# Rows of the later expert slots fetched from DRAM by token number, in place of one-hot gathers on TensorE

## The reference, cut to what matters

```python
def moe_ffn(h, router, w1, w3, w2):
    logits = (h @ router).astype(jnp.float32)
    top_v, top_i = lax.top_k(logits, TOP_K)              # TOP_K = 2
    top_w = jax.nn.softmax(top_v, axis=-1)
    gates = jnp.sum(jax.nn.one_hot(top_i, N_EXPERTS) * top_w[..., None], axis=-2)
    y = gates[..., 0:1] * swiglu(h, w1[0], w3[0], w2[0])
    for e in range(1, N_EXPERTS):
        y = y + gates[..., e:e + 1] * swiglu(h, w1[e], w3[e], w2[e])
    return y                                              # swiglu: (silu(h@w1) * (h@w3)) @ w2
# the caller: h = rmsnorm(x, g_ffn[1]); x = x + moe_ffn(h, ...); return rmsnorm(x, g_final)
```

## Time and profile before

| | |
|---|---|
| median of 3 runs | 1487.76 us (1483.42 to 1487.79) |
| profiled execution | 1485.04 us, of which the span of instructions is 1482.6 us |
| granted TensorE clock | 0.999 of full speed |
| TensorE matmul busy | 1463.4 us (99% of the span) |
| VectorE, ScalarE, GpSimd busy | 895.5, 712.8, 20.6 us |
| DMA over the span | 471.40 MB, mean 318 GB/s |
| queue of the expert weights, whole span | 78.9% of 16 engines |

### The profile page before, as it was taken

The page is one execution under the profiler, slowest core; times in us unless marked ns, Lnnn a source line. Parts: engine busy times, 40 slices in busy tenths (PEclk is TensorE's granted clock), DMA queues, the critical chain, the costliest instruction groups (busy, mean ns, idle before and its releaser), DMA issues.

```text
span 1482.6 us, 19448 instructions
## 1 busy us (share of the span) xinstructions
PE 1463.4 (99%) x7738; PEld 1096.6 (74%) x7738; DVE 895.5 (60%) x901; ACT 712.8 (48%) x752; POOL 20.6 (1%) x39
## 2 busy tenths in 40 slices
PE   9999999999999999999999999999999999999997
PEld 8888889999998888853588834688634888888633
DVE  5856776555457577740399700798402997998402
ACT  5564645434353646420387500677202876877201
POOL 2000000000000000000000000000000000000000
PEclk9999999999999999999999999999999999999999
DMA  9654455555475544799999999999999999999896
GB/s 327 226 163 157 162 179 171 188 182 195 147 248 186 173 165 143 266 408 426 427 426 427 426 426 426 427 427 426 427 427 426 426 427 427 412 379 358 344 427 288
DMA packets 106977, 471.40 MB, mean 318 GB/s; under 512 B 7932, under 2 KB 12160, under 8 KB 63888
## 3 DMA queue, kind: packets, MB, share of 16 engines
q1 hardware_dynamic: 103664, 460.11, 78.9%
q0 software_dynamic: 2656, 9.51, 2.0%
q10 hardware_dynamic: 576, 0.61, 0.1%
HBM read 469.15 MB, written 2.10 MB: 318 GB/s over the span
## 4 chain that ended last, share of the span: by engine, by line
PE 86%; DMA 8%; ACT 2%; SPq 2%; DVE 1%; issue 1%; DVEq 0%; POOL 0%; POOLq 0%
PE big L1900 13%; PE big L1895 13%; PE big L1896 13%; PE big L2459 11%; DMA eraw<-experts 7%; PE small L1895 5%; PE small L1896 5%; PE small L1900 5%; PE big L1974 4%; PE big L1981 4%; PE big L1975 4%; PE small L2002 2%; PE small L2459 2%; SPq L667 1%; PE big L2355 1%; DMA raw<-w_gate 1%
## 5 line engine op out<-in xcount | busy, mean ns | idle before, releaser
L1275 DVE TENSOR_TENSOR elo<-eraw,ehi 128x2048 fp32r<-128x2048 f32 x168 | 379.9, 2288 | 49.3 <-ACT ehi L1006 35.3
L1006 ACT ACTIVATE ehi<-eraw 128x2048 fp32r<-128x2048 f32 x164 | 314.5, 1919 | 128.3 <-PE small L1900 59.5
L1179 DVE TENSOR_TENSOR wlo<-raw,whi 128x2048 fp32r<-128x2048 f32 (+2 forms) x104 | 229.8, 2217 | 136.8 <-ACT whi L784 135.9
L784 ACT ACTIVATE whi<-raw 128x2048 fp32r<-128x2048 f32 (+2 forms) x103 | 190.8, 1857 | 223.7 <-PE big L1900 79.8
L2459 PE MATMUL big<-eraw,he 128*64 128x512 f32 (+1 forms) x1024 | 196.6, 541 | 0.5 <-DVE he L1795 0.5
L1895 PE MATMUL big<-ehi,hehi 128*128 128x512 f32 x448 | 176.0, 393 | 1.9 <-ACT ehi L1003 1.9
L1896 PE MATMUL big<-ehi,helo 128*128 128x512 f32 x448 | 174.4, 389 | 0.0
L2459 PEld LDWEIGHTS big<-eraw,he 128*64 128x64 f32 x1024 | 71.7, 137 | 116.5 <-issue 107.5
L1895 PE MATMUL big<-whi,hhi 128*128 128x512 f32 (+1 forms) x384 | 152.1, 396 | 0.0
L1896 PE MATMUL big<-whi,hlo 128*128 128x512 f32 (+1 forms) x384 | 149.0, 388 | 0.0
L1852 DVE TENSOR_TENSOR hid<-hid,big 128x512 f32<-128x512 f32 (+1 forms) x16 | 9.9, 621 | 195.2 <-PE big L2459 195.2
(11 more groups left out here) (375 smaller groups left out, 1828.2 us busy)
## 6 DMA issues: line engine op xcount, KB each, us to landing
eraw<-experts SPq DMA_DIRECT2D x336, 1024.0 KB, 20.2
raw<-ffn_w SPq DMA_DIRECT2D x30, 1024.0 KB, 5.0
raw<-w_gate SPq DMA_DIRECT2D x24, 1024.0 KB, 5.0
raw<-w_in SPq DMA_DIRECT2D x19, 1024.0 KB, 5.3
raw<-w_branch SPq DMA_DIRECT2D x12, 1024.0 KB, 5.0
raw<-w_o SPq DMA_DIRECT2D x8, 1024.0 KB, 5.0
raw<-w_in SPq DMA_DIRECT2D x4, 896.0 KB, 10.5
gbias<-b_gate POOLq DMA_DIRECT2D x12, 256.0 KB, 4.6
```

The lines of the kernel that those rows point to most:

```text
L784: act.activation(whi[u % HI][:, 0:kt, 0:cols], raw[u % RAW][:, 0:kt, 0:cols], ACT.Copy).then_inc(hi_ready, 1)
L1006: act.activation(ehi[HI_OF[n]][:, :], eraw[n % RING][:, :], ACT.Copy).then_inc(ehi_ready, 1)
L1179: dve.tensor_tensor(wlo[u % RAW][:, 0:kt, 0:cols], raw[u % RAW][:, 0:kt, 0:cols], whi[u % HI][:, 0:kt, 0:cols].bitcast(F32), ALU.subtract) ...
L1275: dve.tensor_tensor(elo[n % RING][:, :], eraw[n % RING][:, :], ehi[HI_OF[n]][:, :].bitcast(F32), ALU.subtract).then_inc(elo_ready, 1)
```

## The change

- ScalarE writes xn = X * nrs (the normalised rows) in two instructions, one per block of 128 tokens, before it takes the exponents.
- GpSimd copies the 256 rows of `xn` (1 MB) to a DRAM tensor `xrows`.
- Slot 0 is gathered as before (`first_gather`). For each later slot: `Gm` is now plain one-hot (is_equal alone). After n = 26 (`NUMBERED`) TensorE multiplies `Gm` with a column of token numbers (`rows_numbered`), into `small[:, 2, 0:1]`: the number of the token at each place, and 0 for a place without a token. At n = 28 VectorE turns them into integers (`numbers_taken`, `rowi`). GpSimd then issues an indirect DMA (`rows_in`), which fetches the rows with these numbers from `xrows` into `xs`, which is `xn[:, 0, :]`: 64 rows for slots 2 and 4, 128 rows for slots 1, 3, 5, 6 and 7.
- `gather` waits for that DMA and then makes 8 transposes of 128 features each.
- Results are added into `X` (there is no `ACC`), and the last normalisation goes into `xn`, from where it is written out.
- TensorE waits for `rows_ready` before it writes bank 2 of `small` at n = 31.

```diff
@@ -113,7 +113,8 @@
-PICKED, GATED, GATES_TURNED, GATES_TAKEN = 24, 1, 36, 41
+PICKED, NUMBERED, NUMBERS_TAKEN = 24, 26, 28
+GATED, GATES_TURNED, GATES_TAKEN = 1, 36, 41
 HE = 2 * PAIRS - 1
...
@@ -376,7 +378,7 @@
         GT32 = at("GT32", over_mask + 6144, [SLOT, NB, P])
-        ACC = xn
+        xs = xn[:, 0, :]
         place[0] = work + o
@@ -395,6 +397,8 @@
         gcol = keep("gcol", [P, 1])
+        mark = keep("mark", [P, 1])
+        rowi = keep("rowi", [P, 1], I32)
         need = keep("need", [P, NM])
...
@@ -542,6 +552,8 @@
+        xrows = nc.dram_tensor("xrows", [TOKENS, D], F32, kind="Internal")
         w_in, w_gate, w_branch, w_o = ins["w_in"], ins["w_gate"], ins["w_branch"], ins["w_o"]
@@ -678,7 +690,7 @@
                 sp.wait_ge(x_ready, 12 + 2 * b + 2)
-                sp.dma_start(out[0, b * P:(b + 1) * P, 512:1024], X[:, b, 512:1024]).then_inc(out_done, 16)
+                sp.dma_start(out[0, b * P:(b + 1) * P, 512:1024], xn[:, b, 512:1024]).then_inc(out_done, 16)
             sp.wait_ge(out_done, 16 * 2 * NB)
@@ -738,6 +750,27 @@
+            for b in range(NB):
+                pool.wait_ge(xn_ready[b], 1)
+                pool.dma_start(xrows[b * P:b * P + P, :], xn[:, b, :]).then_inc(rows_out, 16)
+            pool.tensor_tensor(mark[:, :], eps[:, :], eps[:, :], ALU.add).then_inc(marked, 1)
+            def rows_in(s):
+                n = CAP if is_light(s) else SLOT
+                pool.indirect_dma_start(xs[0:n, :], None, xrows[:, :],
+                                        bass.IndirectOffsetOnAxis(ap=rowi[0:n, 0:1], axis=0)).then_inc(xs_in, 16)
+            pool.wait_ge(rows_out, 16 * NB)
+            for s in range(1, LOOP + 1):
+                pool.wait_ge(rows_ready, s)
+                rows_in(s)
+            pool.wait_ge(routed, 1)
+            last = pool.value_load(metai[0:1, SLOTS:SLOTS + 1], min_val=NE - 1, max_val=SLOTS - 1)
+            with pool.Fori(LOOP + 1, last + 1) as s:
+                pool.wait_ge(marked, s - LOOP)
+                pool.wait_ge(rows_ready, s)
+                pool.tensor_tensor(mark[:, :], eps[:, :], eps[:, :], ALU.add).then_inc(marked, 1)
+                rows_in(s)
@@ -1118,6 +1151,10 @@
             act.activation(nsd[:, 3, :], nvar[:, 3, :], ACT.Sqrt, scale=1.0 / D, bias=eps[:, :]).then_inc(sd_ready, 1)
+            act.wait_ge(rs_ready, 4)
+            for b in range(NB):
+                act.activation(xn[:, b, :], X[:, b, :], ACT.Copy, scale=nrs[:, 3, b:b + 1]).then_inc(xn_ready[b], 1)
             act.wait_ge(lmax_ready, 1)
@@ -1147,14 +1184,14 @@
                 part = slice(512 * half, 512 * half + 512)
-                a = act.activation(X[:, b, part], ACC[:, b, part], ACT.Square, accum_out=nss[:, 4, half, b:b + 1])
+                a = act.activation(xn[:, b, part], X[:, b, part], ACT.Square, accum_out=nss[:, 4, half, b:b + 1])
                 if half:
...
                 act.wait_ge(x_ready, 12 + 2 * b + 1)
-                act.dma_start(out[0, b * P:(b + 1) * P, 0:512], X[:, b, 0:512]).then_inc(out_done, 16)
+                act.dma_start(out[0, b * P:(b + 1) * P, 0:512], xn[:, b, 0:512]).then_inc(out_done, 16)
             act.wait_ge(out_done, 16 * 2 * NB)
@@ -1634,8 +1671,14 @@
                 for b in range(NB):
-                    i = dve.tensor_scalar(Gm[:, b, :], iota, cq[:, 0, b:b + 1], nrs[:, 3, b:b + 1], ALU.is_equal, ALU.mult)
+                    i = dve.tensor_scalar(Gm[:, b, :], iota, cq[:, 0, b:b + 1], None, ALU.is_equal)
                 i.then_inc(picked_ready, 1)
+            def numbers_taken(s):
+                dve.wait_ge(numbered, s)
+                dve.tensor_copy(rowi[:, :], small[:, 2, 0:1]).then_inc(rows_ready, 1)
@@ -1670,10 +1713,9 @@
                     dve.wait_ge(spread_done, 2 * s + b + 1)
-                old = X if isinstance(s, int) and s == 0 else ACC
                 for half in range(2):
                     part = slice(512 * half, 512 * half + 512)
-                    i = dve.tensor_tensor(ACC[:, b, part], old[:, b, part], big[half][:, 1, :], ALU.add)
+                    i = dve.tensor_tensor(X[:, b, part], X[:, b, part], big[half][:, 1, :], ALU.add)
                 i.then_inc(final_added if final else spread_added, 1)
@@ -1684,6 +1726,8 @@
                     picked(s + 1)
+                if n == NUMBERS_TAKEN and not final:
+                    numbers_taken(s + 1)
                 if n in SPREAD_ADDED and not (isinstance(s, int) and s == 0):
...
@@ -1880,7 +1924,7 @@
                 for part in (slice(0, 512), slice(512, 1024)):
-                    dve.scalar_tensor_tensor(X[:, b, part], ACC[:, b, part], nrs[:, 4, b:b + 1], gfin[:, part], ALU.mult,
+                    dve.scalar_tensor_tensor(xn[:, b, part], X[:, b, part], nrs[:, 4, b:b + 1], gfin[:, part], ALU.mult,
                                              ALU.mult).then_inc(x_ready, 1)
@@ -2343,17 +2387,34 @@
+            def first_gather():
+                pe.wait_ge(picked_ready, 1)
+                for j in range(2):
+                    for k in range(4):
+                        for b in range(NB):
+                            f = (4 * j + k) * P
+                            i = pe.matmul(big[j][:, 1, CAP * k:CAP * k + CAP], X[:, b, f:f + P], Gm[:, b, 0:CAP], start=b == 0,
+                                          stop=b == NB - 1)
+                    i.then_inc(gather_done, 1)
+            def rows_numbered(s):
+                pe.wait_ge(picked_ready, s + 1)
+                for b in range(NB):
+                    i = pe.matmul(small[:, 2, 0:1], Gm[:, b, :], tab[:, T_TOK + b:T_TOK + b + 1], start=b == 0, stop=b == NB - 1)
+                i.then_inc(numbered, 1)
             def gather(s, rows):
-                pe.wait_ge(picked_ready, s + 1)
+                pe.wait_ge(xs_in, 16 * s)
                 if not (isinstance(s, int) and s < 2):
...
                     for k in range(4):
-                        for b in range(NB):
-                            f = (4 * j + k) * P
-                            i = pe.matmul(big[j][:, 1, rows * k:rows * k + rows], X[:, b, f:f + P], Gm[:, b, 0:rows], start=b == 0,
-                                          stop=b == NB - 1)
+                        f = (4 * j + k) * P
+                        i = turn(big[j][:, 1, rows * k:rows * k + rows], xs[0:rows, f:f + P], rows)
                     i.then_inc(gather_done, 1)
@@ -2409,6 +2470,10 @@
                     i.then_inc(eunit_done, 1)
+                    if n == NUMBERED:
+                        pe.wait_ge(alo_ready, HE * wides_before(s) + 3)
+                        rows_numbered(s + 1)
                     if n == GATES_TURNED:
@@ -2420,6 +2485,9 @@
                             pe.wait_ge(gt_ready, s)
+                        elif t == 4:
+                            pe.wait_ge(rows_ready, s + 1)
                         if t == HE - 1:
@@ -2463,6 +2531,10 @@
                     d.then_inc(eunit_done, 1)
+                    if n == NUMBERED and not final:
+                        pe.wait_ge(light_taken, PAIRS * i + 2)
+                        rows_numbered(s + 1)
                     if n == GATES_TURNED:
@@ -2474,12 +2546,15 @@
                                 pe.wait_ge(gt_ready, s)
+                            elif p == 2 and not final:
+                                pe.wait_ge(rows_ready, s + 1)
                             for j in range(light_width(p) // P):
...
-            gather(0, CAP)
+            first_gather()
             for s in range(LOOP):
@@ -2523,6 +2598,7 @@
+    t[:, T_TOK:T_TOK + NB] = i[:, None] + P * np.arange(NB)[None, :]
     t[:, T_SUM:T_SUM + NE] = i[:, None] % COLS == np.arange(NE)[None, :]
```

More of the change, by code:

```diff
@@ L157 @@
 T_SUM = T_SIN + NB * ROPE // 2
-T_W = T_SUM + NE
+T_TOK = T_SUM + NE
+T_W = T_TOK + NB
 MIX_UNITS = 34
@@ L512, in encoder @@
         picked_ready = sem("picked_ready")
+        xn_ready = [sem(f"xn_ready{b}") for b in range(NB)]
+        rows_out = sem("rows_out")
+        numbered = sem("numbered")
+        rows_ready = sem("rows_ready")
+        marked = sem("marked")
+        xs_in = sem("xs_in")
         light_turned = sem("light_turned")
@@ L1871, in _ @@
                 dve.wait_ge(end_spread, i + 1)
-                part = ACC[:, b, 512 * half:512 * half + 512]
+                part = X[:, b, 512 * half:512 * half + 512]
                 dve.tensor_tensor(part, part, big[half][:, b, :], ALU.add).then_inc(end_added, 1)
```

## The result

The changed kernel took 1490.67 us (median of 12 runs, 1487.44 to 1502.75); the kernel before, run beside it, 1485.11 us. The ratio is 1.0046 (95% interval 1.0025 to 1.0067). The forecast was 1490.2 us with a range of 1484.5 to 1497.0. So the time lies 0.5 us from the forecast, and the loss is real. What has to be tested is whether the reasons hold.

What follows compares the result with a forecast made beforehand. Bytes were taken to bound the kernel up to slot 5, TensorE behind it. -4.5 us from TensorE and +6.9 from DMA gave +2.4 on 1485.04 (1487.4), plus 2.7 to the median: 1490.2 us, range 1484.5 to 1497.0.

Steps and rivals of the forecast that it cites:

- What bounds the kernel: Bytes at 427 GB/s set the pace up to slot 5's first unit (1143.6 us), TensorE behind it.
- TensorE's saving: Cheaper gathers save 2.25 us a slot, counting only in slots 5 and 6: -4.5 us (3.6 to 5.4).
- The bytes: Copies and gathers in the saturated stretch make slot 5 start 6.9 us later (4.9 to 9.8).
- the price taken half-way to POOL's queue: 1.4 us per 128 fetched rows, between 1.23 at the weights' rate and 1.63 at the POOL queue's rate.
- The copies: Writing `xn` to DRAM at about 647 to 652 us: 2.8 us, partly hidden in unused time, so +1.3 (0 to 3.3).
- What lies beside: Waits for numbers, descriptors and landing rows cost nothing: 27.1 us are left in wide slots, 18.6 in light ones.
- Behind slot 5: Gathers for slots 6 and 7 (2 x 1.4 us) fit into 18.7 us of unused transfer time: no cost.
- Rival 1: Added packets fill gaps left at 427 GB/s, slot 5 starts on time: 1483.3 us; chance 0.08.
- Rival 2: A fetched row costs DMA engines far more than a copied one, at twice the price 1498.6 us; chance 0.20.
- its threshold of 1.75: Price in us per 128 rows from which the kernel would be measurably slower.
- Rival 3: VectorE shuts GpSimd out while descriptors are made, rows come late; at 35 us, 1506.0 us; chance 0.07.
- The marks: Signs: 0.9 us transposes, DMA share 1.01, slot 5 near 1150 us, TensorE idle 5 us before it, POOL up 4.2 MB.

Runs made afterwards that it cites:

- nofetch: The changed kernel without the copy to DRAM and without any fetch, transposes reading rows of tokens 0 to 127: 1482.31 us.
- slowpe: The changed kernel with the eight transposes of the gathers for slots 1 to 5 made four times over: 1491.06 us.
- hybrid: The changed kernel with one-hot gathers from `xn` for slots 1 to 5, fetches for slots 6 and 7 only, copy put off to slot 5: 1481.52 us.
- double: The changed kernel with each fetch issued twice, the second into the other half of `xn`: 1499.16 us.
- hot: The changed kernel with all row numbers made 0, so each fetch reads the same 4 KB repeatedly: 1490.53 us.
- distinct: The changed kernel with each place's row number replaced by the place's own number, so all rows differ and are in order: 1489.18 us.
- halfrow: The changed kernel with plain loads of 128 rows of 2 KB into all 128 partitions for slots 1 to 5: 1485.44 us.
- alldirect: The changed kernel with each indirect fetch replaced by a plain load of the same number of rows: 1490.63 us.

## Why the prediction was right, and where it was not

**The number: closer than the sum deserved.** The 1490.2 us add +2.4 to 1487.76 us, the median of three executions of the kernel before. Twelve executions beside the changed kernel gave 1485.11. So the base was 2.65 us too high and the loss 3.2 us too low (5.6 by the medians; by the ratio, into which the three long executions count, 6.8, with an interval of 3.7 to 10.0), and the two misses offset each other. Inside the profiled execution the stage accounts for +3.0, near the sum's +2.4; the other 2.6 us of the spans stand ahead of the first gather and are not explained.

**What bounds the kernel: right.** Two pieces, bytes up to slot 5 and TensorE behind it. nofetch and slowpe show both sides of the first piece: cheaper gathers leave the pair at 207, and 11.9 us more of TensorE's work leaves it at 210. The second piece is 244.7 to 244.8 us in hybrid, nofetch, double and slowpe, whatever happens ahead of it.

**TensorE's saving: right, a little high.** Forecast 2.25 us a slot, measured 4.23 / 2 = 2.12. The chain of waits after, the view that gave the forecast's prices, has the numbering (forecast 0.45) and the eight transposes (0.87) of slot 6:

```profile
1352.91 0.34 PE small L2406 x4
...
1380.68 0.88 PE big L2046 x8
```

By these a slot would save 3.57 - 0.34 - 0.88 = 2.35 us, so neither price was too low, and where the 0.2 us to the measured 2.12 go is not shown.

**The bytes: near in the sum, by errors that offset each other.** Forecast +6.9 us up to slot 5; measured 2.15 + 2.77 + 2.71 = +7.6. The step that failed is the one that counted rows: 128 + 64 + 128 + 64 + 128 = 512 rows as four blocks of 1.4 us. A block of 128 rows costs 1.26 us, its bytes at the full rate (1.23), so the price taken half-way to POOL's queue was too dear. And a block of 64 rows is no half of it but 1.28 us: there are five blocks, not four, 3 x 1.26 + 2 x 1.28 = 6.3 us for 5.6. The copies cost 0.9 for 1.3. That makes 7.2; the 0.4 us left are within what pairs differ by from run to run (209.8 to 210.4 among the kernels with 64-row fetches). The section of the Trainium skill on the ports, named above, would have given the fifth block; I read the earlier trace rows for the price of a byte and did not ask where the bytes land. The forecast's range also had no case for an execution that runs at 388 GB/s for 100 us: 1498.78 and 1502.75 lie above its 1497.0, though the median hardly moves with them.

**What lies beside: right.** Rows land after 9.7 us (forecast 9.9 to 13.3) of the 18.6 that a light slot leaves. VectorE waits 1.47 us for the numbers ahead of its copy in slot 1, as costed (1.3):

```profile
811.98 0.16 DVE L1681 CAST rowi<-small 128x1 int32<-128x1 f32 x1 [1.47 <-PE small L2406]
```

**Behind slot 5: right.** The fetches for slots 6 and 7 cost nothing (hybrid against nofetch), and slot 7 moved with slots 5 and 6; the end is 0.4 us shorter, not longer.

**Rival 1, bytes absorbed: refuted.** They cost 7.6 us up to slot 5 in the profile, and the medians of hybrid and nofetch lie 9.2 and 8.4 us under that of the changed kernel. **Rival 2, a fetched row is dear: refuted as put** (hot and distinct have the same pair; 1.26 us for 128 rows is under its threshold of 1.75), with a grain of truth in the 64-row blocks at 1.28 us for half the rows. **Rival 3, rows late: its mechanism is real and its effect nil.** GpSimd makes a fetch in 0.94 us in light slots and in 2.7 us in wide ones, where VectorE's subtractions with two SBUF inputs run; 5.8 us were allowed for, and 27.1 us were free. The Trainium skill ("SBUF — State Buffer", section "Who interferes with whom") says that such a VectorE instruction and a GpSimd one that reads SBUF contend, by an exclusive lock; the trace agrees: the fetch begun at 812.41 us ended at 815.14, 0.8 us after the first of two subtractions of 2.29 us that began at 812.05. The plain transfers of halfrow and alldirect, which read no numbers, were made in 0.52 to 0.58 us beside the same subtractions.

**The marks.** The DMA share stayed at 1.01, the eight transposes took 0.88 us in the chain (forecast about 0.9), the queue of POOL took 4.2 MB more (2.8% of 1488.2 less 2.0% of 1482.6 us is 12 us, 1.5 us for each 0.52 MB). Slot 5 came at 1153.87, 3.9 us later than the 1150 named: 2.6 of these are the start of that execution. The idle time of TensorE, forecast as 5 us or more ahead of slot 5, came apart, 0.5 us at each of the last light units and 1.59 us at the start, since TensorE overtakes the loads already inside the light slot.

## What to carry to other kernels

Ask of each stretch which resource ends it, and move work only into the stretch where the other one is idle: the same edit is worth +2.7 us a pair before slot 5 and -2.1 us a slot behind it, and the version that makes it only behind (1481.52 us) beats both kernels. Price an added transfer into saturated engines by the partitions that it fills as well as by its bytes: here 64 rows of 4 KB took the time of 128, and long slow stretches came only with such fetches. When a number comes out right, look at the base and at the terms apart, by marks inside one execution; here a base that was too high hid part of the loss, and two wrong terms offset each other.

## What the hardware showed that was not expected

- With a 64-row fetch in the stream of weights, 16 engines at a share of 1.01 moved 416 to 418 GB/s over 40 us for 426 to 427, the packets of the weights took longer beside it too, and in some executions 388 GB/s for 100 us, worth 8 to 10 us of the time (two of them profiled).
- The clock of TensorE is not the same in all executions of one kernel. Stretches of nofetch where slot 0 starts, and then those of before:

```profile
640.00:645.00 5.00, 4.08 (x23) 2.04 (x23) 2.88 (x12) 1.53 (x5) 0.00 (x0) 1.00 1.00 421
645.00:650.00 5.00, 4.93 (x32) 4.74 (x33) 1.61 (x9) 4.71 (x6) 0.00 (x0) 0.77 1.03 429
650.00:655.00 5.00, 4.48 (x18) 3.19 (x19) 1.90 (x11) 0.72 (x1) 0.00 (x0) 0.50 0.75 315
655.00:660.00 5.00, 5.00 (x20) 1.54 (x18) 4.47 (x31) 0.00 (x0) 0.00 (x0) 0.71 0.37 113
```

```profile
640.00:645.00 5.00, 4.08 (x23) 2.04 (x23) 2.88 (x12) 2.81 (x6) 0.00 (x0) 1.00 1.02 429
645.00:650.00 5.00, 4.93 (x42) 4.74 (x42) 1.61 (x9) 1.96 (x3) 0.00 (x0) 1.00 1.02 428
650.00:655.00 5.00, 4.48 (x25) 1.78 (x25) 4.05 (x26) 0.00 (x0) 0.00 (x0) 1.00 0.93 341
655.00:660.00 5.00, 5.00 (x26) 1.61 (x24) 4.55 (x30) 0.60 (x1) 0.00 (x0) 1.00 1.00 378
```

Both ran the same routing part, busy 4.08 of 5 us. In nofetch the granted clock then fell to 0.50, the level of 1.2 GHz, and the first gather took 6.18 us for 3.79, the first 88 matmuls 21.35 us for 19.10, and slot 1 began 86.56 us after the first gather for 82.03. An execution with the fall has a mean clock of 0.994 to 0.996 for 0.998 or 0.999, and hybrid's medians by it are 1483.8 and 1480.5 us. Executions of both kinds are among those of every kernel here, so this blurs a median of few runs by 3 to 4 us, which is the size of the effects studied here; the pairs of slots inside one execution are free of it.
